# Output projection of the first two branches done in half-tile units between the steps of the mLSTM scan

## The reference, cut to what matters

```python
h_lf, _ = _mlstm_scan(ql, kl, vl, li_f, lf_f, st_f, True)
h_lb, _ = _mlstm_scan(flip(ql), flip(kl), flip(vl), flip(li_b), flip(lf_b), st_b, True)
h_lat = _rms_norm(h_lf + flip(h_lb), g_hd).reshape(B_, S, C_WIDTH)
y_c = jax.nn.sigmoid(co) * h_lat * jax.nn.silu(cz)
y_a = _gmlp_branch(au, av, az, w_s, b_s)
x = x + gt[:, None] * (jnp.concatenate([y_a, y_b, y_c], axis=-1) @ w_out)
```

## Time and profile before

| | us |
|---|---|
| median of 3 runs | 4459.12 (4457.89 to 4460.91) |
| the profiled execution, its own time | 4464.07 |
| its span, first to last instruction | 4462.3 |
| PE busy in the span | 4065.1 (91%) |
| DVE / ACT / POOL busy | 1808.5 / 1340.7 / 639.3 |
| layer 0: first scan matmul to the last POOL product | 917.1 to 1022.3 |
| layer 0: output stage | 1022.5 to 1189.6 |
| layer 1: first scan matmul to the last POOL product | 1970.9 to 2059.3 |
| layer 1: output stage | 2059.5 to 2233.4 |

### The profile page before, as it was taken

One profiled execution on the slowest core, in us unless ns is written; L12 is line 12 of the kernel. 1 busy time (PEld: TensorE's weight loads), 2 busy tenths in 40 slices (PEclk: granted clock), 3 DMA queues, 4 the chain that ended last, 5 costly groups with the idle time before them and its releaser, 6 DMA issues.

```text
span 4462.3 us, 47918 instructions
## 1 busy us (share of the span) xinstructions
PE 4065.1 (91%) x17556; PEld 2292.5 (51%) x17556; DVE 1808.5 (41%) x4027; ACT 1340.7 (30%) x3310; POOL 639.3 (14%) x847
## 2 busy tenths in 40 slices
PE   5989899998989999998999998899999999968995
PEld 3444566674444466655546666544666644433331
DVE  2443456273243455355335655301333310343445
ACT  2323455122132344312334444311222211211122
POOL 1012000021002100002003434200222200002331
PEclk8999999958999999976999999999999999979998
DMA  5010210022200122011210002000111100149885
GB/s 220 1 43 19 76 39 30 2 72 76 78 24 20 68 103 105 2 53 53 85 36 16 27 17 84 19 38 17 39 38 40 45 19 38 52 177 383 320 308 229
DMA packets 88197, 347.25 MB, mean 78 GB/s; under 512 B 20992, under 2 KB 52360, under 8 KB 69152
## 3 DMA queue, kind: packets, MB, share of 16 engines
q1 hardware_dynamic: 69536, 305.35, 18.4%
q0 software_dynamic: 18432, 38.85, 2.5%
HBM read 401.72 MB, written 37.83 MB: 99 GB/s over the span
## 4 chain that ended last, share of the span: by engine, by line
PE 82%; DVE 6%; ACT 4%; issue 4%; DMA 2%; POOL 1%; SPq 0%; POOLq 0%; DVEq 0%; ACTq 0%
PE psum L88 46%; PE psum L94 7%; PE psum L1865 5%; PE psum L3048 4%; PE psum L880 4%; PE psum L859 4%; PE psum L3070 2%; PE psum L2092 2%; DMA arena<-hn_scratch,arena 1%; ACT arena L941 1%; PE psum L1256 1%; PE psum L301 1%; PE psum L2049 1%; ACT arena L1330 0%; PE psum L1796 0%
## 5 line engine op out<-in xcount | busy, mean ns | idle before, releaser
L88 PE MATMUL psum<-arena 128*128 128x512 f32 (+4 forms) x5280 | 2076.7, 552 | 62.3 <-issue 15.4
L88 PEld LDWEIGHTS psum<-arena 128*128 128x128 f32 x5280 | 994.4, 193 | 1065.1 <-issue 993.6
L94 PE MATMUL psum<-arena 128*128 128x128 f32 (+1 forms) x2866 | 457.5, 287 | 123.8 <-ACT arena L941 26.3
L94 PEld LDWEIGHTS psum<-arena 128*128 128x128 f32 (+1 forms) x2866 | 333.7, 144 | 315.3 <-issue 189.2
L1865 PE MATMUL psum<-arena 128*128 128x512 f32 (+1 forms) x640 | 288.5, 578 | 7.7 <-DVE arena L1893 4.4
L3048 PE MATMUL psum<-arena 128*64 x512 | 232.8, 609 | 24.4 <-issue 12.7
L3049 PE MATMUL psum<-arena 128*64 128x512 f32 x512 | 232.8, 609 | 0.0
L175 DVE SCALAR_TENSOR_TENSOR arena<-psum,arena 128x512 f32<-128x512 f32 (+1 forms) x100 | 60.6, 606 | 402.5 <-ACT arena L172 402.0
L170 ACT ACTIVATE arena<-psum 128x512 f32<-128x512 f32 (+1 forms) x100 | 53.0, 530 | 505.7 <-PE psum L88 505.7
L880 PE MATMUL psum<-arena 128*64 128x128 f32 x2624 | 202.5, 283 | 0.7 <-ACT arena L941 0.7
L941 ACT ACTIVATE arena<-psum 128x512 f32<-128x512 f32 x200 | 112.7, 596 | 252.1 <-PE psum L94 251.9
(11 more groups left out here) (413 smaller groups left out, 4725.3 us busy)
## 6 DMA issues: line engine op xcount, KB each, us to landing
arena<-w_gu SPq DMA_DIRECT2D x32, 2048.0 KB
arena<-w_ada SPq DMA_DIRECT2D x24, 2048.0 KB
arena<-w_dn SPq DMA_DIRECT2D x32, 1024.0 KB
arena<-w_in SPq DMA_DIRECT2D x12, 2048.0 KB
arena<-w_out SPq DMA_DIRECT2D x6, 2048.0 KB
arena<-gate_rows_scratch SPq DMA_DIRECT2D x36, 256.0 KB, 3.3
x_scratch<-arena SPq DMA_DIRECT2D x18, 512.0 KB, 2.9
arena<-x SPq DMA_DIRECT2D x16, 512.0 KB, 10.2
```

Of the source, the lines that this page charges most:

```text
L88: ins = e.matmul(out, l, r, start=(i == 0), stop=(i == n - 1))
L94: ins = e.transpose(o, i, idn)
```

## The change

Of the projection, the six blocks of branches a and b (columns 0 to 767 of `Y`) move out of the output stage and in among the steps of the scan. A unit is half a tile (512 output columns): unit i belongs to tile i // 2 and half i % 2. `both_ways` now calls two hooks in each step: `first`, behind the first part of step i, and `second`, at the end of the round.

- PE: `pe_first` runs three of the unit's six matmul blocks (`pe_po`, part 0), `pe_second` the other three. Between them it turns the six blocks of the tile (`pe_po_turn`: two in `pe_first` of an even i, four in `pe_second` of an odd i). ACT copies them to `yS` (`a_po_copy`).
- DVE: `v_po` multiplies the unit before by the gate and writes it over columns 0 to 767 of `Y` and into `ext` (one instruction of 512 columns for an even unit, two of 256 for an odd one).
- The gate rows are made ahead of the scan and in its first step (`pe_gate_rows`, `v_gate_diag`, `a_gate_rows`).
- Output stage: PE turns two blocks instead of eight and each product runs over two blocks instead of eight (k = 6, 7). POOL, which had nothing here, adds the residual row to `Y` and `ext` (`g_out`: 768 and 256 columns). DVE adds that sum; its second addition of a tile is two instructions of 256. DVE's copy of turned blocks is gone. Residual rows are asked for once POOL, not DVE, is done with their buffer.
- Buffers are laid out anew, so that gates and `ext` live through both stages.

```diff
+        def pe_po(e, l, i, part):
+            m, t, g = po_unit(l, i)
+            w = weight(("out", l, g), 512)
+            if part == 0:
...
+                e.wait_ge(*acop.of("yS", l, m, 0))
+                if g:
+                    e.wait_ge(*acop.of("yS", l, m, 1))
...
+            for k in range(3 * part, 3 * part + 3):
+                ins = e.matmul(P[7] if g else P[3], yS[:, m % 2, k, :], w[:, k, :], start=(k == 0), stop=(k == 5))
...
+        def v_po(e, l, i):
...
+            if g == 0:
+                e.tensor_tensor(Y[:, t, 0:512], P[3], gtr[:, v, 0:512], ALU.mult).then_inc(*vmul.by("po", l, i))
...
+                e.tensor_tensor(Y[:, t, 512:768], P[7][:, 0:256], gtr[:, v, 512:768], ALU.mult)
+                e.tensor_tensor(ext[:, t, :], P[7][:, 256:512], gtr[:, v, 768:1024], ALU.mult).then_inc(*vmul.by("po", l, i))
...
+        def pe_first(e, l, i):
+            if i == 0 and l == 0:
+                pe_gate_rows(e, l, 1)
+            if po_unit(l, i):
+                m, t, g = po_unit(l, i)
+                pe_po(e, l, i, 0)
+                if g == 0:
+                    pe_po_turn(e, l, m, 1)
+
+        def pe_second(e, l, i):
+            if po_unit(l, i):
+                m, t, g = po_unit(l, i)
+                pe_po(e, l, i, 1)
+                if g and po_unit(l, i + 1):
+                    pe_po_turn(e, l, m + 1, 0)
...
+        def a_first(e, l, i):
+            if i == 0 and l == 0:
+                a_gate_rows(e, l, 1)
+            if po_unit(l, i) and i % 2 == 0:
+                a_po_copy(e, l, i // 2, 1)
+
+        def a_second(e, l, i):
+            if i % 2 and po_unit(l, i + 1):
+                a_po_copy(e, l, i // 2 + 1, 0)
...
-        def both_ways(step):
+        def both_ways(step, first, second_):
...
-                    for x in (a, b, a, b, c):
+                    next(a, None)
+                    first(2 * n + d)
+                    for x in (b, a, b, c):
                         next(x, None)
+                    second_(2 * n + d)
...
-                mm(e, out_bank(n, g), [(yT[:, k, tile(ts[n])], w[g][:, k, :]) for k in range(8)]
+                e.wait_ge(*acop.of("y", l, ts[n]))
+                mm(e, out_bank(n, g), [(yT[:, k, tile(ts[n])], w[g][:, k, :]) for k in (6, 7)]
...
+        def g_out(e, l):
+            for t in tiles_of(l):
+                i = t % 2
+                e.wait_ge(*rows_in[2 + i].of("res", l, t))
+                e.tensor_tensor(Y[:, t, 0:768], Y[:, t, 0:768], xr[:, i, 0:768], ALU.add)
+                e.tensor_tensor(ext[:, t, :], ext[:, t, :], xr[:, i, 768:1024], ALU.add).then_inc(*gmul.by("res", l, t))
...
-                        e.wait_ge(*rows_in[2 + i].of("res", l, t))
+                        e.wait_ge(*gmul.of("res", l, t))
                         e.wait_ge(*vmul.of("outg", l, t, g))
-                        e.tensor_tensor(xo[:, i, half(g)], xo[:, i, half(g)], xr[:, i, half(g)], ALU.add
-                                        ).then_inc(*vmul.by("outx", l, t, g))
-                    if n + 2 < len(ts):
-                        y_copy(n + 2)
+                        if g == 0:
+                            e.tensor_tensor(xo[:, i, 0:512], xo[:, i, 0:512], Y[:, t, 0:512], ALU.add
+                                            ).then_inc(*vmul.by("outx", l, t, g))
+                        else:
+                            e.tensor_tensor(xo[:, i, 512:768], xo[:, i, 512:768], Y[:, t, 512:768], ALU.add)
+                            e.tensor_tensor(xo[:, i, 768:1024], xo[:, i, 768:1024], ext[:, t, :], ALU.add
+                                            ).then_inc(*vmul.by("outx", l, t, g))
```

More of the change, by code:

```diff
@@ L1135, in sp_gates, with po_unit, po_blocks, pe_po_turn @@
                                     ).then_inc(*nm_in[2 * d + n % 2].by(l, d, n))
+        def po_unit(l, i):
+            ts = tiles_of(l)
+            return (i // 2, ts[i // 2], i % 2) if i < 2 * len(ts) else None
+        def po_blocks(m, part):
+            return (P[3] if m else P[7], 0, 4) if part == 0 else (P[7], 4, 6)
+        def pe_po_turn(e, l, m, part):
+            b, k0, k1 = po_blocks(m, part)
+            if part == 0 and m:
+                e.wait_ge(*vmul.of("po", l, 2 * m - 2))
+            elif part:
+                e.wait_ge(*(vmul.of("po", l, 2 * m - 1) if m else acop.of("gate_row", l, len(gates_of(l)) - 1, 1)))
+            turn(e, [(b[:, tile(k - k0)], Y[:, tiles_of(l)[m], tile(k)]) for k in range(k0, k1)], ident
+                 ).then_inc(*turned.by("yS", l, m, part))
@@ new lines, in gates_of, with pe_gate_rows, v_gate_diag @@
+        def gates_of(l):
+            return [1, 0] if l == 0 else [0]
+        def pe_gate_rows(e, l, n):
+            for q in range(2):
+                e.wait_ge(*vsta.of("gate_row", l, n, q))
+                e.wait_ge(*(acop.of("gate_row", l, n - 1, q) if n else acop.of("yS", l, 0, 0)))
+                e.matmul(P[7 if q else 3], ones, dg[:, q].rearrange("p a b -> p (a b)"), start=True, stop=True
+                         ).then_inc(*prod.by("gate_row", l, n, q))
+        def v_gate_diag(e, l, n):
+            for q in range(2):
+                if n:
+                    e.wait_ge(*prod.of("gate_row", l, n - 1, q))
+                cols = MODs[l][:, 16 + 4 * q:20 + 4 * q, gates_of(l)[n]]
+                e.tensor_tensor(dg[:, q], mid(ident, 4), bc(cols, 128), ALU.mult).then_inc(*vsta.by("gate_row", l, n, q))
@@ new lines, in a_gate_rows @@
+        def a_gate_rows(e, l, n):
+            for q in range(2):
+                e.wait_ge(*prod.of("gate_row", l, n, q))
+                e.activation(gtr[:, gates_of(l)[n], half(q)], P[7 if q else 3], ACT.Copy).then_inc(*acop.by("gate_row", l, n, q))
+        def pe_first(e, l, i):
[6 more added lines that the diff above has]
+                    pe_po_turn(e, l, m, 1)
@@ L1137, in v_gates, with v_first @@
+        def v_first(e, l, i):
+            if i == 0 and l == 0:
+                v_gate_diag(e, l, 1)
+            if i and po_unit(l, i - 1):
+                v_po(e, l, i - 1)
         def v_gates(e, l):
@@ L1161, in v_gates @@
             e.wait_ge(*vmul.of("state", l, 2))
+            e.wait_ge(*turned.of("maxima", l))
+            v_gate_diag(e, l, 0)
         def a_gates(e, l):
+            a_po_copy(e, l, 0, 0)
             for c0 in range(0, NT, 4):
@@ L1524, in pe_out @@
                     e.wait_ge(*vmul.of("norm", l + 1, u))
-                    if before is None:
-                        e.wait_ge(*acop.of("y", l, ts[1]))
-                        e.wait_ge(*vcop.of("y", l, ts[1]))
-                        if l == 0:
-                            e.wait_ge(*acop.of("gate_row", l, 1, 1))
-                    else:
+                    if before is not None:
                         e.wait_ge(*acop.of("norm", l + 1, before))
@@ L1542, in y_copy @@
             def y_copy(n):
-                e.wait_ge(*turned.of("y", l, ts[n], 0))
-                e.activation(yT[:, 0:4, tile(ts[n])], y_bank(n, 0).rearrange("p (j x) -> p j x", j=4), ACT.Copy
+                e.wait_ge(*turned.of("y", l, ts[n]))
+                e.activation(yT[:, 6:8, tile(ts[n])], y_bank(n)[:, 0:256].rearrange("p (j x) -> p j x", j=2), ACT.Copy
                              ).then_inc(*acop.by("y", l, ts[n]))
```

120 lines of the change are left out of this document (51 added, 69 removed).

## The result

The changed kernel takes 4479.23 us (median of 5 runs, 4476.45 to 4482.77), the kernel before, run beside it on the same chip, 4460.32 (4457.89 to 4462.3). The ratio is 1.0043, with a 95% interval of 1.0031 to 1.0054: 19 us slower. Its profiled execution has a span of 4474.7 us against 4462.3, at a mean granted clock of 0.949 against 0.937.

A forecast was written before the change was run, and what follows sets the result against it. PE was taken to bound the output stage and about two thirds of scan steps, DVE and ACT's exchange the rest. Scans +67.6, +64, +8, output stages -70.5, -56.5 gave +12.6 us: median about 4471, own range 4455 to 4490, ends 4436 and 4508.

The forecast's parts named there:

- Clock in the scan: Both scans: PE's clock rises from 0.50 to the full level within the first units and stays.
- never rises: Rival, scan: the clock stays at the lower level, 31 steps of 15.4 us, +238, 4709 us; chance 0.05.
- own matmuls keep their pace: Rival, scan: its own matmuls stay at 4.4 us a step whatever the clock, 4539 us; chance 0.04.
- Step: Scan: a step with a unit takes 7.73 us on PE, which bounds it, plus 0.25 allowed for waits.
- Heads: Scan starts: layer 0's reaches 936.7 instead of 921.17 (+15.5 us), layer 1's 2009 instead of 1977.27 (+32).
- Scans: Both scans together: +140 us, from +67.6 in layer 0, +64 in layer 1 and +8 for waits.
- Output stage of layer 0: 96.6 us against 167.1, -70.5; first tile scaled at 19.5 us, period 8.2 us.
- Output stage of layer 1: 117.4 us against 173.9, -56.5; period 11.6 us, first tile 15.1 including 3.5 for the second context tile.
- Holds: Output stages: POOL's residual additions hold DVE's second addition, giving periods 8.2 instead of 6.6 and 11.6 instead of 9.45 us.
- POOL and DVE don't meet: Rival, output stages: residual rows land late, periods stay 6.6 and 9.45, 33 us less, 4438; chance 0.22.
- falls back now and then: Rival: clock drops in scan waits or output-stage pauses, DVE waits for PE, some 25 us, 4496; chance 0.20.
- Sum: Whole kernel: +67.6 + 64 + 8 - 70.5 - 56.5 = +12.6 us on the profiled execution, 4476.7; median about 4471.

The follow-up runs named there:

- filler: Changed kernel plus six unread 256-column matmuls per tile in PE's queue where it would idle, in layer 1's output stage; 4480.73 us, ratio 1.0039 to the kernel before.
- The run with added work: Kernel with only the gate rows moved, plus two unread 512-column matmuls per scan step from the fifth to the twentieth; 4466.82 us, ratio 1.0005 to the kernel before.
- the run with half units: Changed kernel with only every second tile moved, three of a unit's six matmuls to a step; 4424.36 us, ratio 0.9913 to the kernel before.
- the residual on DVE: Changed kernel with the whole residual added by DVE one tile ahead, POOL unused in the output stage; 4460.46 us, ratio 0.9997 to the kernel before.
- PE's order repaired: All tiles moved, DVE adding the residual; in layer 1 the small turn follows the second product, the first context tile's 32-column product comes earlier; 4442.6 us, ratio 0.9965.
- POOL's additions narrow: Changed kernel with POOL adding the residual to only 8 columns of each piece, leaving out the rest; 4453.67 us, ratio 0.9981 to the kernel before.

## Why the prediction was right

The forecast was 4471 with a range of 4436 to 4508 and slower as the likeliest sign; measured 4479.23. Point by point:

- **Clock in the scan.** Right: 0.98 and 1.00, from 924 and 1975 on. The rivals "never rises" and "own matmuls keep their pace" fell: 2.36 us a step for the forecast 2.25.
- **Step.** 7.73 and 0.25 of waits were forecast; measured, from 936.44 (second part of step 0) to 1084.22 (step 18), 8.21. The allowance was near in size and wrong in kind: in most steps PE waits for nothing, and what is added lies in the matmuls (a unit 5.45 for 5.15, own 2.36 for 2.25, turns 0.75 a pair of steps for 0.66, from start to start). Only single waits, such as 0.54 and 0.59 us for an ACT copy, came on top.
- **Heads.** 936.7 forecast, 936.44 measured; 2009 forecast, 2010.41 measured.
- **Scans.** +140 forecast; the pieces give +74.7 and +68.4, 143.1.
- **Output stage of layer 0.** -70.5 forecast, -75.8 measured with all up to the next gates. The first tile's scaling ends 18.1 us in (forecast 19.5), periods are 7.9 instead of 8.2. The working of the first tile had slips that hid each other: its terms add up to 16.5 and not 16.9, and from the addition's end to the scaling's end give 3.7 us and not the 2.6 between 16.9 and 19.5.
- **Output stage of layer 1.** -56.5 forecast, -52.8 measured. The first tile came as forecast (24.7 us in for 25.1). The periods of 11.5 and 11.8 are the forecast 11.6, but in part by luck: only in two of the seven are they made by holds alone. In three, DVE waits 1.5 to 1.8 us for PE and is held about 0.5, and the forecast had no wait for PE there. With the holds gone the period is 9.5 or 11.0, not 9.45 throughout. One interval is 17.0 us: the order of PE behind ACT, which I had put at 3.5 in the first tile and nothing later.
- **Holds.** Shown by removing them: period 6.55, 25.3 us over the four pieces. I had reckoned 1.6 and 2.15 a tile and 4 for the first tiles, 33. The rival "POOL and DVE don't meet" fell.
- **Clock in the output stages.** The rival "falls back now and then" came true there in the clock (0.83 and 0.75), and DVE did wait for PE in layer 1. It did not cost the 25 us of the rival: filler, which raised the clock, gained nothing, since the holds stood behind the steady waits, and the long wait went with PE's order.
- **Sum.** +12.6 forecast for the profiled execution, +12.4 in its span. So close a meeting is luck: the scans cost 3.5 us more than forecast, layer 0's output stage and what follows gave 5.3 more, layer 1's gave 3.7 less, and "rest" took 2.0 off. The ratio says 19. The profile's "rest" is 2.0 us shorter than before; among the fourteen profiles of this study it lies anywhere between 3131.9 and 3140.8, and some us of each median may come from there. What moves it was not looked into.

Why so large a move gives so little is now plain. Of 36 units each costs PE 5.45 us and its turns wherever they stand. In the output stages PE gave them up, and the chain of DVE, ACT and POOL became the bound. In the middle of the scan a step took 4.43 us, and PE at full clock needs 2.36 of them for the step's own matmuls. Some 2 us a step were free, less than half a unit. The run with added work put 1.8 us there and kept the step's length; the run with half units put 2.8 there and made the step 5.24 us. How short a step the exchange with DVE and ACT alone would allow in the middle of the scan isn't shown, and no run moves just what fits.

## What to carry to other kernels

Ask of work that is to be moved how much of it the receiving place can take for nothing, and move that much; against the changed kernel, moving half the units gave -1.3%, where moving all of them gave -0.46% with the residual on DVE and -0.78% with PE's order repaired as well. When the donor stage stops being bound by one engine, look at once at what its other engines wait for and in which order they stand. A wait can hide another one behind it: filler took DVE's steady waits for PE away, and DVE met POOL's holds instead. Look at what stands behind a wait before you pay for its removal.

## What the runs showed of the hardware

A busy PE did not mean a fast PE: in the same stretch of two kernels that differ in the added matmuls alone, PE was busy 75.24 of 80 us at a clock of 0.94 with two 512-column matmuls a step, and 75.17 of 80 us at 0.53 without them. The Trainium skill ("TensorE: Matmul & The Clock Gate", section "Why this matters for your kernels") asks for a busy TensorE; the trace doesn't bear that out, since both were as busy and only one had the clock.

POOL also holds a DVE instruction with a single input. In the changed kernel, DVE's scaling of a context tile, 0.75 us alone, took 1.52 beside POOL's 768 columns, which had begun 0.85 us before it (timelines of both):

```profile
2134.59 1.82 POOL L1681 TENSOR_TENSOR arena<-arena 128x768 f32<-128x768 f32 x1 [7.58 <-DMA arena<-x_scratch]
...
2135.44 1.52 DVE L1697 TENSOR_SCALAR arena<-arena 128x1024 f32<-128x1024 f32 x1 [0.51 <-ACT arena L1642]
```

With POOL's additions narrow the same instruction takes 0.76. The prediction had counted only instructions with two inputs. The Trainium skill ("SBUF — State Buffer", section "Who interferes with whom") does name such one-input instructions, in DVE's faster modes, beside those with two. The trace agrees that this one was held (1.52 for 0.75 us); in which mode it ran, no run shows.
